# Front of a hybrid encoder block: x loaded transposed and split unnormalised, the norm's gain put onto the weights and its root onto the results

## The reference, cut to what matters

```python
def rmsnorm(x, g):
    y = xf * lax.rsqrt(jnp.mean(xf * xf, axis=-1, keepdims=True) + EPS)
    return y * g

h = concat([meta, x])                  # T = 16 + 1024 tokens, D_MODEL = 1024
hn = rmsnorm(h, norm_mix_g)
proj = hn @ w_in                       # 1024 x (512 x_lru, 512 g_lru, 256 c_q, 128 c_kv, 32 k_pe)
xc = dwconv(x_lru, ...)                # 4 taps along the tokens
y_lru = rg_lru_bidir(xc, ...) * gelu(g_lru)     # gates r, i from xc @ small matrices, two scans
q = rmsnorm(c_q, q_latent_g) @ w_uq    # per head rmsnorm, rope; kv likewise from c_kv, k_pe
...                                    # attention, output projection, ConvGLU FFN: untouched
```

## Time and profile before

| | |
|---|---|
| time, median of 3 runs | 1296.12 us (1292.5 to 1298.64) |
| the profiled execution's own time | 1296.43 us |
| its span, first to last instruction | 1294.3 us |
| granted TensorE clock, mean over the span | 0.997 |
| PE busy over the span | 1271.2 us, 98% |
| DVE, ACT, POOL busy | 998.4, 769.7, 147.8 us |

### The profile page before, as it was taken

One profiled execution on the slowest core, in us unless ns is written; L12 is line 12 of the kernel. 1 busy time (PEld: TensorE's weight loads), 2 busy tenths in 40 slices (PEclk: granted clock), 3 DMA queues, 4 the chain that ended last, 5 costly groups with the idle time before them and its releaser, 6 DMA issues.

```text
span 1294.3 us, 18581 instructions
## 1 busy us (share of the span) xinstructions
PE 1271.2 (98%) x6202; PEld 1020.5 (79%) x6202; DVE 998.4 (77%) x1507; ACT 769.7 (59%) x1154; POOL 147.8 (11%) x175
## 2 busy tenths in 40 slices
PE   7999999999999999999999999999999999999997
PEld 7999998866667666687678888888888888888886
DVE  6677569778887886576879878787878887787855
ACT  7487648577766875633455565647465565646461
POOL 3000037400000001322300000000010001000010
PEclk9999999999999999999999999999999999999999
DMA  6011200000000024200234657566584746576567
GB/s 222 34 54 41 74 1 1 1 1 9 10 10 9 10 64 150 90 9 25 77 119 98 163 113 163 130 177 127 133 185 90 179 106 162 125 168 135 148 152 238
DMA packets 40939, 123.02 MB, mean 95 GB/s; under 512 B 7378, under 2 KB 8082, under 8 KB 34484
## 3 DMA queue, kind: packets, MB, share of 16 engines
q0 software_dynamic: 7200, 52.43, 21.4%
q1 hardware_dynamic: 33684, 69.86, 15.5%
HBM read 62.34 MB, written 59.80 MB: 94 GB/s over the span
## 4 chain that ended last, share of the span: by engine, by line
PE 84%; DVE 7%; ACT 4%; DMA 2%; issue 2%; SPq 0%; POOL 0%; DVEq 0%; ACTq 0%
PE banks L2960 31%; PE banks L3032 15%; PE banks L100 7%; PE banks L102 7%; PE banks L101 7%; PE banks L1954 2%; PE banks L2060 2%; PE banks L2104 2%; PE banks L2061 2%; PE banks L2107 2%; PE banks L2062 2%; PE banks L2105 2%; ACT e_f L1567 1%; PE banks L1909 1%; PE banks L1933 1%
## 5 line engine op out<-in xcount | busy, mean ns | idle before, releaser
L2960 PE MATMUL banks<-x_hi,slot_h 128*128 128x512 f32 x616 | 242.9, 394 | 2.7 <-DVE slot_l L2648 1.5
L2960 PE MATMUL banks<-x_lo,slot_h 128*128 128x512 f32 x616 | 243.4, 395 | 0.0
L2960 PE MATMUL banks<-x_hi,slot_l 128*128 128x512 f32 x616 | 242.9, 394 | 0.0
L2433 ACT ACTIVATE slot_h<-up_raw 128x512 fp32r<-128x512 f32 x127 | 79.9, 630 | 174.1 <-PE banks L2960 169.1
L2960 PEld LDWEIGHTS banks<-x_hi,slot_h 128*128 128x128 f32 x616 | 115.6, 188 | 31.4 <-DVE slot_l L2648 2.6
L2960 PEld LDWEIGHTS banks<-x_lo,slot_h 128*128 128x128 f32 x616 | 115.7, 188 | 27.0
L2960 PEld LDWEIGHTS banks<-x_hi,slot_l 128*128 128x128 f32 x616 | 115.7, 188 | 26.9
L2511 ACT ACTIVATE staged<-banks 128x1024 f32<-128x1024 f32 x100 | 101.6, 1026 | 40.9 <-PE banks L3032 40.9
L3032 PE MATMUL banks<-dn_h,a_h 128*128 128x512 f32 x280 | 110.4, 394 | 0.0
L3032 PE MATMUL banks<-dn_h,a_l 128*128 128x512 f32 x280 | 109.5, 391 | 0.0
L3032 PE MATMUL banks<-dn_l,a_h 128*128 128x512 f32 x280 | 109.5, 391 | 0.0
(11 more groups left out here) (357 smaller groups left out, 2866.9 us busy)
## 6 DMA issues: line engine op xcount, KB each, us to landing
down_sums<-staged POOLq DMA_DIRECT2D x50, 1024.0 KB, 8.0
up_raw<-in_w_up SPq DMA_DIRECT2D x88, 256.0 KB, 3.6
dn_raw<-in_w_down SPq DMA_DIRECT2D x22, 512.0 KB, 6.8
win_raw<-in_w_in SPq DMA_DIRECT2D x11, 512.0 KB, 3.4
x_tm<-in_x_tm SPq DMA_DIRECT2D x8, 512.0 KB, 6.0
wo_raw<-in_w_out SPq DMA_DIRECT2D x16, 256.0 KB, 4.4
h<-in_x_tm SPq DMA_DIRECT2D x8, 512.0 KB, 5.5
down_sums<-h SPq DMA_DIRECT2D x3, 1024.0 KB, 7.1
```

The lines of the kernel that those rows point to most:

```text
L2433: nc.scalar.activation(s_h[slot], x, ACT.Copy).then_inc(sem["up_hi"], 1)
L2960: ins = nc.tensor.matmul(o, s[slot][:, k], xs[w], start=fresh and k == 0 and n == 0, stop=k == 3 and n == 2, skip_group_check=not fresh)
```

## The change: what it does

- **x arrives twice.** Once transposed by the host (`x_raw`, features on partitions, chunk by chunk; the first chunk in two halves of four feature blocks), which is rounded and subtracted as it is, with no norm (`high_x`, `low_part`; chunks 2 and 3 wholly on DVE, `high_low_x`). Once with tokens on partitions (`x_tm`, in four pairs of tiles), only for the sums of squares (`square_x`). The transposes by PE, `scale_x` and the broadcast load of the gain are gone.
- **The gain** goes onto the rows of each of the 12 weight tiles, by one POOL `tensor_tensor` of 128x1024 (`gain_w`, x12, the k tile 128x256), which sits between the tile's DMA and `high_w`. The first two stand ahead of `softplus` on POOL, the others behind it.
- **The root.** After the nine squares one `var_x`, one `std_x` and `diag_x`: the identity times r for all eight tiles in one DVE operation of 128x1024. PE multiplies ones by these diagonals (`rows_of_r`, nine matmuls, three units R), which gives r along the free axis on all partitions; ACT copies it to SBUF (`copy_r`, `x_rb`).
- **Reads.** x and g units are no longer read by ACT but by DVE, times `x_rb` (`read_scaled`, 13 reads of x units, 12 of g units). gelu is then one ACT operation of 1040 columns out of SBUF for each g tile. c units are not multiplied: their own norms take the root out, with eps scaled by the variance (`v_kv_eps`, `v_q_eps`).
- **Order.** PE starts with 28 products of the identity (`warm`) and then goes straight to the units of x0 and c0, in 8 different banks. The banks of all later units move.

```diff
+    raw_at = (M_LRU, M_YL, M_YL + 2 * P * KD, M_LRU + (META + 2 * P) * KD)
+    x_raw = [place(f"x_raw{c}", at, (KD, 2 * P + (0 if c else META))) for c, at in enumerate(raw_at)]
...
-    bank_no = [n % 4 for n in range(len(first_units))] + [(4 + n) % 8 for n in range(shared)] +\
+    bank_no = list(range(len(first_units))) + [1, 3, 5] + [(AT + n) % 8 for n in range(shared)] +\
...
+        def gain_w(n):
+            cols = ROPE if tiles[n][0] == "k" else P
+            pool.wait_ge(sem["w_in"][n % 3], 16 * (n // 3 + 1))
+            w = w_raw[n % 3][:, :, 0:cols]
+            nc.gpsimd.tensor_tensor(w, w, mix_g.unsqueeze(2).broadcast_to((P, KD, cols)), ALU.mult).then_inc(sem["w_gain"], 1)
+
+        pool.wait_ge(sem["par_in"], 16)
+        gain_w(0)
+        gain_w(1)
         softplus()
+        for n in range(2, len(tiles)):
+            gain_w(n)
...
         def high_w(n):
-            act.wait_ge(sem["w_in"][n % 3], 16 * (n // 3 + 1))
+            act.wait_ge(sem["w_gain"], n + 1)
...
+        def copy_r():
+            for c, (c0, cn) in enumerate(((META, 4 * P), (META + 4 * P, 4 * P), (0, META))):
+                wait_unit(act, ("R", 0, c))
+                nc.scalar.activation(x_rb[:, c0:c0 + cn], ps(("R", 0, c))[:, 0:cn], ACT.Copy).then_inc(sem["read_act"], 1)
...
         def gelu(f):
-            if f:
-                act.wait_ge(sem["y_lru"], f)
-            for c, (c0, cn) in enumerate(CH):
-                wait_unit(act, ("g", f, c))
-                nc.scalar.activation(gel[:, c0:c0 + cn], ps(("g", f, c))[:, 0:cn], ACT.Gelu_apprx_tanh)\
-                  .then_inc(sem["read_act"], 1)
+            wait_read(act, ("g", f, 2))
+            nc.scalar.activation(gel, gel, ACT.Gelu_apprx_tanh).then_inc(sem["gelu"], 1)
...
+        def high_low_x(c):
+            c0, cn = LOAD_CH[c]
+            dve.wait_ge(sem["xr_in"][c - 2], 32)
+            for w in range(2):
+                link(nc.vector.tensor_copy(xn_h[:, HALVES[w], c0:c0 + cn], x_raw[c][:, HALVES[w]]))
+                low_part(c, w)
+
+        def low_part(c, w):
+            c0, cn = LOAD_CH[c]
+            nc.vector.tensor_tensor(xn_l[:, HALVES[w], c0:c0 + cn], x_raw[c][:, HALVES[w]],
+                                    f32(xn_h[:, HALVES[w], c0:c0 + cn]), ALU.subtract).then_inc(sem["x_lo"], 1)
...
+        def read_scaled(u, out):
+
+            c0, cn = chunk(u)
+            wait_unit(dve, u)
+            nc.vector.tensor_tensor(out, ps(u)[:, 0:cn], x_rb[:, c0:c0 + cn], ALU.mult).then_inc(sem["read_dve"], 1)
...
         recurrence(0)
+        read_x(2)
         for c in range(3):
             low_c(1, c)
...
         recurrence(1)
         low_w(7)
+        read_x(3)
         for c in range(3):
             low_c(2, c)
...
-        for j in range(3):
-            warm(j)
-            transpose_x(j)
-        warm(3)
+        pe.wait_ge(sem["ident_in"], 16)
+        warm(28)
         for c in range(len(LOAD_CH)):
-            pe.wait_ge(sem["x_lo"], 2 * c + 3)
             project(("x", 0, c))
-            if 2 * c + 4 < NL:
-                transpose_x(2 * c + 4)
             project(("c", 0, c))
+        pe.wait_ge(sem["set_up"], 3)
+        rows_of_r()
```

More of the change, by code:

```diff
@@ L166, in front_phase @@
     kpe_fm = place("kpe_fm", M_KPE, (T,), parts=ROPE)
[L168 to L172, removed]
+    raw_at = (M_LRU, M_YL, M_YL + 2 * P * KD, M_LRU + (META + 2 * P) * KD)
+    x_raw = [place(f"x_raw{c}", at, (KD, 2 * P + (0 if c else META))) for c, at in enumerate(raw_at)]
+    x_sb = [place(f"x_tm{b}", at, (2, D)) for b, at in
+            enumerate((M_C + T, M_C + 4 * T, M_CSQ + T, raw_at[3] + 2 * P * KD))]
+    x_meta = place("x_meta", M_KPE, (D,), parts=META)
+    assert raw_at[3] + 2 * P * KD + 2 * D <= M_C and M_KPE + 3 * T <= WORDS
+    x_rb, x_dg = place("x_rstd_rows", M_KPE + T, (T,)), place("x_diag", M_KPE + 2 * T, (XT, P))
+    x_dgm = place("x_diag_meta", M_KPE + 2 * T + SEQ, (META,), parts=META)
+    x_var, x_r = stat[:, 0, 0:NT], stat[:, 0, 16:16 + NT]
+    x_std, v_kv_eps, v_q_eps = stat[:, 1, 0:NT], stat[:, 0, 48:48 + NT], stat[:, 1, 48:48 + NT]
+    mix_g = par[:, COLS["mix_g"]:COLS["mix_g"] + KD]
     uq_h = place("uq_h", M_UQ, (2, NQ), F32R)
@@ L557, in scalar @@
         decay(0, lambda: high_gw(1))
-        for c in range(3):
-            read_x(2, c)
         high_w(5)
@@ L567, in scalar @@
         high_w(7)
-        for c in range(3):
-            read_x(3, c)
         for c in range(3):
@@ new lines, in read_scaled, with read_x @@
+        def read_scaled(u, out):
+            c0, cn = chunk(u)
+            wait_unit(dve, u)
+            nc.vector.tensor_tensor(out, ps(u)[:, 0:cn], x_rb[:, c0:c0 + cn], ALU.mult).then_inc(sem["read_dve"], 1)
+        def read_x(f):
+            if f == 0:
+                dve.wait_ge(sem["set_up"], 3)
+                wait_read(dve, ("R", 0, 2))
+            else:
+                dve.wait_ge(sem["conv"], f)
+            for u in units_of("x", f):
+                c0, cn = chunk(u)
+                read_scaled(u, xpad[:, 2 + c0:2 + c0 + cn])
@@ L3165, in _pack @@
         rs[:n, i] = np.concatenate([-sin[t0:t0 + n], sin[t0:t0 + n]], 1)
+    x_fm = np.concatenate([a["meta_tokens"], a["x"][0]], 0).T.reshape(KD, P, T).transpose(1, 0, 2)
+    first_cols = META + 2 * P
+    x_raw0 = np.stack([x_fm[:, KD // 2 * w:KD // 2 * (w + 1), 0:first_cols] for w in range(2)])
+    x_raw = np.stack([x_fm[:, :, first_cols + 2 * P * c:first_cols + 2 * P * (c + 1)] for c in range(3)])
     first = {"x": 0, "g": LRU, "c": 2 * LRU}
```

313 lines of the change are left out of this document (155 added, 158 removed).

## The result

The changed kernel takes 1296.66 us (median of 20 runs, 1294.29 to 1304.69) against 1293.95 for the kernel before (20 runs): a ratio of 1.0021, 95% interval 1.0012 to 1.0030. It is 2.7 us slower. The profiled execution has a span of 1295.5 us, against 1294.3.

The account below looks back on a forecast made before the run. PE was taken to bound the kernel (busy 98%, 84% of the chain). Terms -4.7 + 0.4 + 4.6 + 2.0 + 0.7 = +3.0 on 1296.43, 0.3 above the median, gave 1299.1 us; range 1290 to 1306, leaving out 2 in 10.

Parts of the forecast that it names:

- case A: Forecast case: DVE's recurrence, lengthened by gains, holds x3's banks; G2 waits 4 to 7 us; total 0 to +6; chance 0.5.
- x1's start: PE's first unit of x1 starts at 42.0 instead of 46.72, the transposes being gone: -4.7 us.
- G1: PE's gate tile G1 waits for DVE's read of x2 behind recurrence(0), lengthened by a gain pass: +0.4 us.
- G2: PE's gate tile G2 waits for DVE's read of x3 behind recurrence(1), lengthened by a gain pass: +4.6 us.
- clock behind G2's wait: After idling at G2, PE comes back at the slow clock, some 4 us at half speed: +2.0 us.
- The end: From g3 to q: DVE's read, one gelu of 1040 and the table load, 2.9 us, partly hidden: +0.7 us.
- Diagonal ... 39.9: Ahead of R: late softplus delays gain(2), then the squares; reciprocals and the diagonal are done at 39.9 us.
- R's nine products 1.1: Step before x1: PE's nine products that make R take 1.1 us.
- over at about 39: Start: PE idles 3.3 to 4.3 us, runs slow some 5 us, and the first products end at about 39.
- The meeting of POOL and DVE: Each waits for the other's whole operation: gain passes delay DVE up to 2.4 us, DVE operations delay POOL up to 1.3.
- gain pass 2.4: POOL's 128x1024 gain pass on a weight tile takes 2.4 us, a lower bound, lengthening each recurrence by 2.4.
- B: Rival: no meeting, gains fit DVE's pauses; -8.5 us at best, about 1291 (1287.5 to 1294); chance 0.28.
- C: Rival: weights 9's gain gets in too and gain(3) delays the diagonal; +8.7 us, 1305; chance 0.17.

Follow-up runs that it names:

- after: The changed kernel itself, as profiled and timed against the kernel before: 1296.66 us, ratio 1.0021.
- experiment 2: Changed kernel with softplus on POOL moved behind the gain pass of weights 2 instead of ahead of it: 1291.12 us, ratio 0.997.
- experiment 1: Changed kernel with POOL's twelve gain passes left out, so the norm's gain is missing from the result: 1287.75 us, ratio 0.9953.
- 4: Changed kernel with 16 identity products between c0's last unit and R: 1296.66 us, ratio 1.0023.
- experiment 6: Changed kernel with the gain pass in recurrence(0), at 76.7 us, cut to one column of 128: 1296.68 us, ratio 1.0013.
- 5: Changed kernel with ACT instead of DVE reading the 13 x units, without the root on the x branch: 1293.85 us, ratio 0.9999.
- 3: Changed kernel with 36 identity products between c0's last unit and R: 1298.82 us, ratio 1.0036.
- experiment 7: Changed kernel with ACT taking the gelu straight from g's banks, without the root on the gate branch: 1297.52 us, ratio 1.0032.
- 8: Changed kernel with the banks of g3's first and last piece exchanged: 1297.5 us, ratio 1.0018.
- experiment 12: Kernel of experiment 9 with 22 identity products, first weights split ahead of x, weights 2 split behind the roots, g3's last piece in bank 5: 1285.47 us, ratio 0.9932.
- experiment 9: Changed kernel with the norm's gain multiplied onto x during its split on ACT and DVE, POOL multiplying nothing: 1287.63 us, ratio 0.9958.
- experiment 11: Kernel of experiment 9 with 19 identity products, first weights split ahead of x, and g3's first and last banks exchanged: 1288.09 us, ratio 0.9939.

## Why the prediction was right

1299.1 was forecast, 1296.66 came, inside the range of case A (1296 to 1302.5), by case A's mechanism. The forecast stood on a base of 1296.43, 2.5 above the median that 20 runs gave the kernel before; as a change it was +3.0, and +2.7 came. That these lie so close is luck: the start was 2.4 us worse than forecast, G2 with the clock behind it 3.9 better. Term by term, on PE's marks:

| term | forecast | measured |
|---|---|---|
| x1's start | -4.7 | -2.3 |
| G1 | +0.4 | +0.8 |
| G2 | +4.6 | +2.7 |
| clock behind G2's wait | +2.0 | 0 in the profile of after, +1.3 to +1.6 in four others |
| the end | +0.7 | +1.0 |
| between x1 and G1 | 0 | +0.1 |
| sum | +3.0 | +2.3 (first q product) |

**The start.** "Diagonal ... 39.9": R's products began at 40.19, softplus was over at 29.65 (forecast 30), `high_w(2)` stood at 31.67 behind the gain of 29.73. That chain was right, and experiment 2 shows it: softplus moved, R is at 36.3. That it came out to 0.1 us is luck again: ACT was through with the squares at 36.5 (forecast 37.7), and then gain(3), of 36.05, held up DVE's pair on the sums by 1.3 us:

```profile
36.51 1.52 DVE L677 TENSOR_SCALAR stat<-stat 128x8 f32<-128x8 f32 x2 [1.59 <-ACT x_tm L473]
```

This is nearly the bound that the prediction gives, "gain(3) falls into the diagonal and the idle PE slows: 45": x1 came at 44.4.

The step that failed is "R's nine products 1.1". Two errors lie in it. At full clock R takes 2.3 with its small last product (experiments 1 to 4), since a 128-column fp32 product shows as two records, and I had counted each record as a product: the "20 warm products" of the kernel before are 10 in its code. And I looked for the slow clock at the first product, where it did not come, and only as a bound at R, where PE idles 4.6 us: there R took 4.2. The slow clock at the start, "over at about 39", was wrong because the 28 identity products did not "end at 8.6 to 9.6" but at 11.7, for the same reason: PE was idle for 0.5 us and not for 3.3 to 4.3. The first product came at 12.24 for 12.9, behind gain(1) and `low_w(0)` as forecast, and the last at 35.6.

**The meeting of POOL and DVE**, read from a single operation of 1.26 us, holds. softplus stretched from 11.4 to 18.6 us, gain(1) to 2.89 and DVE's `low_w(0)` beside it to 2.92. Reads out of PSUM are free of it. In the changed kernel a pass of 1.90 runs beside them:

```profile
117.63 1.90 POOL L401 TENSOR_TENSOR win_raw<-win_raw,par 128x1024 f32<-128x1024 f32 x1 [9.20 <-DMA win_raw<-in_w_in]
```

```profile
116.91 1.36 DVE L698 TENSOR_TENSOR xpad<-banks,x_rstd_rows 128x348 f32<-128x348 f32 x3
118.19 1.54 DVE L730 SCALAR_TENSOR_TENSOR c_l<-banks,par,c_h 128x348 fp32r<-128x348 f32 x3
```

Both groups have the length that they have in experiment 1 without any pass (1.36 and 1.54). By the Trainium skill ("SBUF — State Buffer", SBUF: two separate sides) the lock counts against operations with two SBUF inputs or in a two-port mode; the trace agrees, for the scan and the products in the recurrence as for the reads that go free.

**G1 and G2.** The step "gain pass 2.4" was too long: 1.90, so each recurrence grew by 1.6, not 2.4. Counted from x1, the read of x3 that PE waits for ended 73.0 us later where 74.4 was forecast: 0.8 of this is the shorter delay in recurrence(1), 0.4 its earlier start. And PE wanted the bank at 70.6 for 70.0, since G1 had held it longer. So the wait is 2.5 for 4.5. The mechanism is shown from three sides: without the passes G2 loses 0.3 (experiment 1), without the first of them 0.6 less of wait (6), without the reads it loses 1.2 less (5).

**The clock behind G2's wait** was forecast at 2.0. It fell in the profiles of experiments 2, 3, 4 and 6, and not in those of after, 5, 7 and 8, with nearly the same wait. It costs 1.3 to 1.6 where it comes. What decides it stays open; it explains why experiments 4 and 6 gave back in G2 what they had won ahead of it.

**The end** had the right size for the wrong reason. "g3's last unit is read by DVE, gelu is one operation, then the table load": taking that away gave 0.06 (experiment 7), moving the bank gave 0.98 (experiment 12). I had not followed the shift of the bank numbers to the q products. PE's wait there, 0.81, is one of the signs that the prediction named for being wrong ("where I see 2 us of slack"). By q's third tile 0.57 of the 0.98 is left (18.91 after g3 for 19.48), where DVE's read of the first tile holds it.

**The signs.** Of those named, the first product (12.24), G1's wait (0.5) and DVE operations of up to 3.7 us (3.91) came. x1 at 41 to 43 (44.4), a wait of 4 to 7 us at G2 (2.5) and the clock behind it did not, and the pass took 1.90 alone, less than the 2.4 that was the lower bound. The order of things was right, the sizes were not.

**The rivals.** B, where the meeting costs nothing, is nearest to the kernel without the passes: -8.5 at best was forecast for it, and experiment 1 gave -6.1 by its ratio, -7.1 by the medians. C did not come: weights 9 got their gain at 117.63, behind the recurrence's end at 116.6, as A had it by 1 us. Between the first q product (+2.3) and the end of the span (+1.2) the profile of after gains 1.1 back. It does so in the FFN: its first product with the up weights starts 2.7 later than before (634.3 for 631.6), the last product of the span 0.7 later (1288.8 for 1288.1). Why stays open.

## What to carry to other kernels

Before work goes to an idle engine, ask what it shares with the busy one: here eleven passes of 1.9 us and one of 0.6 on an engine 11% busy turned -6 us into +3, and the same factor put into operands of operations that ran anyway cost PE nothing. When you count products in a timeline, compare the count with the code. A wait on PE has two prices, its own length and the clock after it, so an earlier start is worth something only if the next thing PE waits for comes as early; fill or close the gap, don't open it. After a change in the allocation of banks, look at who now inherits each one, up to the stage behind the change.

## What was not expected of the hardware

- A matmul of 128 fp32 columns shows as two records, which follow each other by 0.11 us at full clock (72 records in 8.0 us for 36 products). R's eight of them take 2.0 us, not 1.0.
- At the start of an execution the identity products' records follow each other by 0.21 us, twice as far apart as later, for 2.9 to 5.9 us (until 6.9 in after, until 10.1 in experiment 9), while the profile's clock column says 1.00.
- A chain of operations of 0.2 us on POOL, each waiting for the one before, is stretched to one for each DVE operation (1.18, 1.13, 1.04 in a row from 11.07 on in the changed kernel).
- DVE's scan is held up like any other operation (3.91 for 2.32), and so are its operations with one SBUF input and a scalar: the pair at 36.51, on 8 columns and on 1, took 1.52 beside the pass of 36.05 (0.21 in experiment 2).
- Waits of 1.88 us (experiment 6) and 1.94 us (experiment 11) were followed by products at half clock, waits of 0.95 and 1.06 us (experiments 1 and 4, at R) were not.
- Two waits of 2.46 and 2.47 us at the same place of the program left the clock at 1.00 in one kernel and at 0.50 in another.
